# An identity product in each squaring, and full-width sums, in the recurrent stage of a hybrid decoder step

## The reference, cut to what matters

```python
def rwkv7_scan(r, decay, k, v, kk, kka, s0):
    def step(s, inp):
        r_t, w_t, k_t, v_t, kk_t, kka_t = inp
        s_kk = jnp.einsum('bhvk,bhk->bhv', s, kk_t)
        s = s * w_t[:, :, None, :] - s_kk[..., None] * kka_t[:, :, None, :] + v_t[..., None] * k_t[:, :, None, :]
        return s, jnp.einsum('bhvk,bhk->bhv', s, r_t)
    xs = tuple(jnp.swapaxes(t, 0, 1) for t in (r, decay, k, v, kk, kka))
    s_final, ys = lax.scan(step, s0, xs)
    return jnp.swapaxes(ys, 0, 1), s_final
```

## Time and profile before

| | us |
|---|---|
| median of 3 runs | 3478.74 |
| lowest, highest | 3476.14, 3480.61 |
| the profiled execution, its own time | 3477.89 |
| its span, first to last instruction | 3476.3 |
| the mean TensorE clock granted in it, of full | 0.943 |
| part of the span from the first `side` to the last (15 rounds) | about 2149.6 to 2624.3 |

### The profile page before, as it was taken

How to read it: one execution, slowest core, us unless ns; L and a number is a source line. 1 busy time by engine, 2 the same in 40 slices (tenths; PEclk the granted TensorE clock), 3 DMA queues, 4 the chain that set the end, 5 groups by cost and what they waited for, 6 DMA issues and landing times. The chain is left out here.

```text
span 3476.3 us, 65264 instructions
## 1 busy us (share of the span) xinstructions
PE 3178.0 (91%) x25272; PEld 1931.4 (56%) x25272; DVE 2175.2 (63%) x4350; ACT 1108.8 (32%) x2329; POOL 553.6 (16%) x782
## 2 busy tenths in 40 slices
PE   8999999999999999879999765877785999999998
PEld 4544445555555555446666544767774555555553
DVE  2018889999999999567666554777773344532221
ACT  4136650000000000145554325666652111111221
POOL 3330000000000000021011133445542000000000
PEclk9999999999999999979999876888877999999999
DMA  5232111121111111232111372222214312121110
GB/s 160 74 97 60 45 39 57 55 63 55 57 57 55 57 55 57 86 78 55 42 38 33 90 228 56 57 54 62 61 30 133 110 53 64 64 77 59 49 40 25
DMA packets 215814, 233.48 MB, mean 67 GB/s; under 512 B 28665, under 2 KB 191028, under 8 KB 215012
## 3 DMA queue, kind: packets, MB, share of 16 engines
q1 hardware_dynamic: 147960, 110.07, 11.7%
q0 software_dynamic: 23696, 59.79, 6.0%
q10 hardware_dynamic: 43868, 59.62, 4.9%
HBM read 158.75 MB, written 70.63 MB: 66 GB/s over the span
## 5 line engine op out<-in xcount | busy, mean ns | idle before, releaser
L409 PE MATMUL fro_acc<-h_t,fro_w 128*128 128x416 f32 x3280 | 1173.6, 515 | 0.0
L409 PEld LDWEIGHTS fro_acc<-h_t,fro_w 128*128 128x128 f32 x3280 | 614.2, 190 | 542.4 <-issue 535.5
L692 DVE TENSOR_SCALAR_CACHE_REDUCE fro_work<-scores,fro_real 128x384 uint8<-128x384 f32 (+6 forms) x462 | 656.2, 1474 | 2.1
L516 ACT ACTIVATE fro_out<-fro_acc 128x416 f32<-128x416 f32 (+3 forms) x230 | 118.0, 513 | 794.1 <-PE fro_acc L409 711.5
L3108 DVE CUSTOM_DVE_ANT_0 att_seen<-att_ps,scores 128x512 f32<-128x512 f32 (+3 forms) x320 | 181.4, 608 | 99.6 <-PE att_ps L2994 99.2
L2172 PE MATMUL mrg_po<-mrg_wo,mrg_mrg 128*128 128x512 f32 (+1 forms) x544 | 238.8, 597 | 4.6 <-DVE mrg_mrg L2277 4.6
L2204 PE MATMUL mrg_pg<-mrg_wg,mrg_x_t 128*128 128x512 f32 (+1 forms) x544 | 236.3, 592 | 0.0
L658 DVE SCALAR_TENSOR_TENSOR scores<-fro_work,w_idx,scores 128x512 f32<-128x512 f32 (+3 forms) x280 | 188.0, 671 | 39.2 <-ACT fro_work L573 12.2
L3078 ACT ACTIVATE att_seen<-att_seen,att_shift 128x128 f32<-128x128 f32 (+15 forms) x128 | 152.6, 1194 | 82.8 <-DVE att_shift L3116 82.8
L2172 PEld LDWEIGHTS mrg_po<-mrg_wo,mrg_mrg 128*128 128x128 f32 (+1 forms) x544 | 101.5, 187 | 139.1 <-issue 134.1
L573 ACT ACTIVATE fro_work<-fro_wk 128x512 f32<-128x512 f32 (+3 forms) x320 | 144.5, 540 | 90.7 <-PE fro_wk L482 89.8
(11 more groups left out here) (445 smaller groups left out, 4556.4 us busy)
## 6 DMA issues: line engine op xcount, KB each, us to landing
z_t<-fro_out ACTq DMA_DIRECT2D x180, 208.0 KB
fro_w<-in_w_in SPq DMA_DIRECT2D x41, 512.0 KB, 4.2
mrg_m_in<-z_t POOLq DMA_DIRECT2D x56, 256.0 KB, 3.3
scores<-in_cache_kv POOLq DMA_DIRECT2D x108, 128.0 KB, 3.2
rwk_zi<-z_t SPq DMA_DIRECT2D x80, 129.0 KB, 2.6
z_t<-fro_out ACTq DMA_DIRECT2D x45, 192.0 KB
scores<-in_x_prompt SPq DMA_DIRECT2D x16, 512.0 KB, 8.5
mrg_x<-in_x_prompt SPq DMA_DIRECT2D x16, 512.0 KB, 3.6
```

Of the source, the lines that this page charges most:

```text
L409: last = pe.matmul(acc[e % 2][:, 0:CW], w[block_no % 3][:, kk, :], h_t[:, kk, CW * g:CW * g + CW], start=(kk == 0), stop=(kk == KD - 1))
L692: chain.mark(dve.tensor_scalar(junk[b % 2][:, 0:n], scores[:, c:c + n], realf[:, b:b + 1], None, op, ALU.add, accum_out=count[:, b:b + 1]))
```

## The change

The sum of product and old series moves from DVE to PE: in `square(m, r)` for r from 1 to 4 each block's four products are followed by four products with `eye` that add the old series into the same place of PSUM. ACT then copies power and series together (`take_square`, 128x512 in place of 128x256), and DVE only transposes. The last series is copied by DVE in one instruction to `diag` (the room of `pw[0]`), transposed from there, and its first half is put into `inv` by a full-width product with a column of ones and zeros (`part`). The second half goes through PE: `corner` copies it by an identity product, and ACT takes both in one instruction. `first_product` is a full-width sum of two halves with such a column on DVE, behind the first transpose, and a full-width sum with the identity on POOL. `grams` now does all of e = 0 and then all of e = 1 with a semaphore after each, and `mask` waits for each half.

```diff
@@ first product
-                pool.wait_ge(masked, 4 * m + 4)
...
-                for i, (x, h) in enumerate(FOURTHS):
-                    w = fourth(x, h)
-                    pool.tensor_tensor(ta[1][w, :, 1, :], lower(gram[m % 2])[w, :, sub(h)], eye[w, None, :].to_broadcast([H, BLK, H]), ALU.add)\
-                        .then_inc(acc1_ok, 1)
-                    pool.wait_ge(acc1_ok, 4 * m + i + 1)
+                pool.wait_ge(acc1_ok, 2 * m + 1)
+                pool.tensor_tensor(ta[1][:, :, 1, :], ta[1][:, :, 1, :], eye[:, None, :].to_broadcast([P, BLK, H]), ALU.add).then_inc(acc1_ok, 1)
@@ grams
-                for i in range(2):
-                    for p2, x, e in HEADS:
-                        p = 2 * p2 + x
...
+                for e in range(2):
+                    if c:
+                        pe.wait_ge(masked, 4 * m + 1 + e)
+                    for i in range(2):
+                        for p2 in range(2):
+                            for x in range(2):
+                                p = 2 * p2 + x
...
+                    last.then_inc(grammed, 1)
@@ square
-                        last = pe.matmul(zz[w, 0, at], by, src, start=True, stop=True)
+                        last = pe.matmul(zz[w, 0, at], by, src, start=True, stop=(r == 0), skip_group_check=True)
+                    if r:
+                        for x, h in FOURTHS:
+                            w = fourth(x, h)
+                            last = pe.matmul(zz[w, 0, 64 * b + H:64 * b + 64], eye[w, :], ta[r % 2][w, b, 1, :], start=False, stop=True,
+                                             skip_group_check=True)
@@ corner
-                        last = pe.matmul(zz[fourth(x, 0), 0, 64 * b + H:64 * b + 64], ta[1][w, b, 0, :], inv[m % 2][w, b, sub(1)],
-                                         start=True, stop=True)
+                        pe.matmul(zz[fourth(x, 0), 0, 64 * b + H:64 * b + 64], ta[1][w, b, 0, :], diag[w, b, :], start=True, stop=True)
+                        last = pe.matmul(zz[w, 0, 64 * b + H:64 * b + 64], eye[w, :], diag[w, b, :], start=True, stop=True)
@@ take_square
+                    act.activation(ta[(r + 1) % 2][:, :, :, :].rearrange("p b i c -> p (b i c)"), zz[:, 0, :], ACT.Copy).then_inc(t_ok, 1)
@@ take_corner
-                for x in range(2):
-                    w = fourth(x, 0)
-                    act.activation(inv[m % 2][w, :, sub(1)], zz[w, 0, :].rearrange("p (b i c) -> p b i c", i=2, c=H)[:, :, 1, :], ACT.Copy)\
-                       .then_inc(inv_ok, 1)
+                if m >= 2:
+                    act.wait_ge(u_ok, NC * (m - 1))
+                act.activation(inv[m % 2][:, :, sub(1)], zz[:, 0, :].rearrange("p (b i c) -> p b i c", i=2, c=H)[:, :, 1, :], ACT.Copy)\
+                   .then_inc(inv_ok, 1)
@@ first_power
                 dve.transpose(pw[0][:, :, :], lower(gram[m % 2])).then_inc(p_ok, 1)
+                if m:
+                    dve.wait_ge(acc_ok, m)
+                dve.scalar_tensor_tensor(ta[1][:, :, 1, :], lower(gram[m % 2])[:, :, sub(1)], part[1][:, :], lower(gram[m % 2])[:, :, sub(0)],
+                                         ALU.mult, ALU.add).then_inc(acc1_ok, 1)
@@ power
-                    if r < 4:
-                        dve.tensor_tensor(ta[(r + 1) % 2][:, :, 1, :], got(r), ta[r % 2][:, :, 1, :], ALU.add).then_inc(acc_ok, 1)
-                        return
...
-                    for x, h in FOURTHS:
-                        w = fourth(x, h)
-                        last = dve.tensor_tensor(inv[m % 2][w, :, sub(h)], got(r)[w], ta[r % 2][w, :, 1, :], ALU.add)
...
+            def last_power(m):
+                dve.wait_ge(sq_ok, 5 * m + 5)
+                dve.tensor_copy(diag, zz[:, 0, :].rearrange("p (b i c) -> p b i c", i=2, c=H)[:, :, 1, :]).then_inc(acc_ok, 1)
+                dve.wait_ge(acc_ok, m + 1)
+                dve.transpose(pw[1][:, :, :], diag).then_inc(flipped, 1)
+                if m >= 2:
+                    dve.wait_ge(u_ok, NC * (m - 1))
+                dve.tensor_scalar(inv[m % 2][:, :, sub(0)], diag, part[0][:, :], None, ALU.mult).then_inc(inv_ok, 1)
```

More of the change, by code:

```diff
@@ L991, in stage_rwkv @@
         mask4, eye = s.sb("mask4", [P, 4 * C]), s.sb("eye", [P, H])
+        part = [s.sb(f"part{i}", [P, 1]) for i in range(2)]
         rheads = s.sb("rheads", [P, 4, P])
@@ L1013, in stage_rwkv @@
         inv = [s.sb(f"inv{i}", [P, BLK, C]) for i in range(2)]
+        diag = pw[0][:, :, 0:H]
         q_tok = [s.sb(f"q_tok{i}", [P, 2, 2, HD]) for i in range(2)]
@@ L1162, in _ @@
             pool.memset(e_in[:, :, :, 0:1], 1.0).then_inc(zeroed, 1)
-            for i in range(2):
-                pool.memset(inv[i][:, :, :], 0.0).then_inc(zeroed, 1)
             def shifted(m, i):
@@ L1336, in grams @@
                         pe.wait_ge(inv_ok, 2 * m)
-                else:
-                    pe.wait_ge(masked, 4 * m + 2)
-                for i in range(2):
-                    for p2, x, e in HEADS:
-                        p = 2 * p2 + x
-                        last = pe.matmul(zz[half_of(x), e, 256 * p2 + P * i:256 * p2 + P * i + P], kbz[half_of(e), i, p, tokens(c)],
-                                         ar[m % 3][half_of(e), p, c, :, :].rearrange("p a c -> p (a c)"), start=True, stop=True)
-                last.then_inc(grammed, 1)
+                for e in range(2):
[5 more added lines that the diff above has]
+                                p = 2 * p2 + x
+                                last = pe.matmul(zz[half_of(x), e, 256 * p2 + P * i:256 * p2 + P * i + P], kbz[half_of(e), i, p, tokens(c)],
+                                                 ar[m % 3][half_of(e), p, c, :, :].rearrange("p a c -> p (a c)"), start=True, stop=True)
+                    last.then_inc(grammed, 1)
             def square(m, r):
@@ L1351, in square @@
                 elif r == 1:
-                    pe.wait_ge(acc1_ok, 4 * m + 4)
-                else:
-                    pe.wait_ge(acc_ok, 4 * m + r - 1)
+                    pe.wait_ge(acc1_ok, 2 * m + 2)
                 low = lower(gram[m % 2])
@@ L1574, in exps @@
                 else:
-                    act.wait_ge(zeroed, 3)
+                    act.wait_ge(zeroed, 1)
                 act.activation(e_in[:, :, :, 1:C + 1], chunked(cum[:, :, :]), ACT.Exp, scale=decay_half()).then_inc(e_ok, 1)
@@ L1610, in take_square @@
                 act.wait_ge(sq_ok, 5 * m + r + 1)
-                act.activation(ta[(r + 1) % 2][:, :, 0, :], zz[:, 0, :].rearrange("p (b i c) -> p b i c", i=2, c=H)[:, :, 0, :], ACT.Copy)\
-                   .then_inc(t_ok, 1)
+                if r == 0:
+                    act.activation(ta[1][:, :, 0, :], zz[:, 0, :].rearrange("p (b i c) -> p b i c", i=2, c=H)[:, :, 0, :], ACT.Copy).then_inc(t_ok, 1)
+                else:
+                    act.activation(ta[(r + 1) % 2][:, :, :, :].rearrange("p b i c -> p (b i c)"), zz[:, 0, :], ACT.Copy).then_inc(t_ok, 1)
             def take_side(m):
@@ L1724, in _ @@
                 chain.mark(dve.tensor_copy(eye[w, :], k.ident[w, w]))
+            for h in range(2):
+                for x in range(2):
+                    for i in range(2):
+                        chain.mark(dve.memset(part[h][fourth(x, i), :], 1.0 if i == h else 0.0))
             for x in range(2):
@@ L1788, in scaled_keys @@
                 if m:
-                    dve.wait_ge(grammed, m)
+                    dve.wait_ge(grammed, 4 * m)
                     dve.wait_ge(kbt_ok, 2 * m)
@@ L1815, in first_power @@
                 dve.transpose(pw[0][:, :, :], lower(gram[m % 2])).then_inc(p_ok, 1)
[L1817 to L1818 removed]
+                if m:
+                    dve.wait_ge(acc_ok, m)
+                dve.scalar_tensor_tensor(ta[1][:, :, 1, :], lower(gram[m % 2])[:, :, sub(1)], part[1][:, :], lower(gram[m % 2])[:, :, sub(0)],
+                                         ALU.mult, ALU.add).then_inc(acc1_ok, 1)
             def power(m, r):
[L1822 to L1841 removed]
+                dve.wait_ge(t_ok, 4 * m + r + 1)
+                dve.transpose(pw[(r + 1) % 2][:, :, 0:H], ta[(r + 1) % 2][:, :, 0, :]).then_inc(p_ok, 1)
+            def last_power(m):
[6 more added lines that the diff above has]
+                dve.tensor_scalar(inv[m % 2][:, :, sub(0)], diag, part[0][:, :], None, ALU.mult).then_inc(inv_ok, 1)
             def take_u(n, c):
@@ L1942, in _ @@
                 if inverse:
-                    power(n + 1, 4)
+                    last_power(n + 1)
                 if features:
```

24 lines of the change are left out of this document (1 added, 23 removed).

## The result

The changed kernel takes 3525.08 us (median of 4 runs, 3514.93 to 3533.77), the kernel before, run beside it, 3479.68 (4 runs). The ratio is 1.0134, with a 95% interval from 1.0108 to 1.0159: 45 us slower, where 27 us faster was predicted. The profiled execution took 3522.3 us.

What follows compares the result with a forecast made beforehand. No engine is full; a round is a loop of waits, chiefly PE's for DVE and POOL. 10.11 + 19.19 = 29.30 us, plus 0.7 for the clock, gives 30.0 against 31.65, 25 us over 15 rounds: 3452 us, range 3428 to 3486.

Steps and rivals of the forecast that it cites:

- the price of the identity products: Squares 1 to 4 on PE: 32 identity products of 32 columns add 0.51 us to each square at full clock.
- M: Start of the mask of the second grams in a round; predicted at S + 10.11, 2.75 us sooner than before.
- The last sum: End of the squares on DVE: four instructions of 1.71 us become one copy of 0.41, so `side` starts at S + 0.95.
- `side` to the second grams: PE's stretch from `side`: 7.61 us with the clock kept; POOL is later and sets M at S + 10.11.
- S: Start of the last sum on DVE, the point from which a round's times are counted.
- Grams: The 16 products of a grams on PE in the new order: 1.94 us at full clock instead of 1.06.
- the rival that rested on it: Products sharing input rows do not run side by side: 16 take 3.6 us, about 3481 us, no change; chance 0.06.
- M to square 1: After the second mask starts: DVE's added sum and POOL's `pm` put the transpose at M + 5.71, square 1 at M + 6.2.
- Square 2: Start of square 2 on PE, behind ACT's wider copy of square 1: M + 11.10, 0.93 us later than before.
- Square 2 to the next S: Squares 2 to 4 at full clock: 6.78 us to square 4, then 1.31, so the next S is M + 19.19.
- The clock: PE's clock over a round: one fall to half in most rounds, 3 us long, taken as 0.7 us lost.
- The slower rival: Half clock stays behind `side` and PE's added work is paid double: 33.2 us a round, 3501 us; chance 0.12.

Runs made afterwards that it cites:

- the wide product: Changed kernel with one full 128x128 identity product over 256 columns replacing the 32 small ones in each of squares 1 to 4: 3449.64 us, ratio 0.9909.
- the one-column products: Kernel before plus 32 products of one column in each of squares 1 to 4, results overwritten before being read: 3575.99 us, ratio 1.0278.
- ident_alone: Kernel before with only the sum of squares 1 to 4 moved to PE, as 32 identity products each, and wide ACT copies: 3541.15 us, ratio 1.0172.
- one_ident_alone: Kernel before with only the sum of squares 1 to 4 moved to PE, as one full-width product each: 3474.06 us, ratio 0.9983.

## Why the prediction was wrong

The step that failed is the price of the identity products: "32 identity products of 32 columns add what a square of 32 columns takes beyond its start and end, 0.75 - 0.24 = 0.51". As the time of their columns that is right (0.50 at full clock where no stop falls in), but I never counted that they are 128 instructions a square, 512 a round. No rival priced instructions either. What the runs showed in its place are 60 stops of some 60 us in all, which go with the instructions. They are paid in the stretch after square 2 as idle time, and where one falls just ahead of `side`, the clock behind it is at half. Of the mean round, 34.3 us against 29.3 worked out at full clock, 2.3 us are lost ahead of M and 2.7 behind it. So the working up to M holds for the rounds that keep their clock and not for the mean.

- *The last sum.* Predicted one copy of 0.41; measured 0.42. By the row of the transpose, PE waited for it ahead of `side` once, 2.5 us at the last one (the waits above call this one "issue"), in place of 33.0 us in 16 rounds.
- *`side` to the second grams.* Predicted to keep its clock, with M at S + 10.11, set by POOL. In the round shown the clock is 1.00 from 2431 to 2436, the bias add ends at S + 3.89 (3.80 predicted), and M is S + 10.37. Ten of the 15 rounds do not keep their clock (0.50 to 0.88), and M is S + 10.6 to 18.4 in these. In the round shown `next_state` starts at 2440.53, 0.08 us after POOL's `keep_state` ended; the profile names PE's output product as the last to release it.
- *Grams.* Predicted 1.94 at full clock; from the first start (2439.88) to the last end it was 1.54. At half clock, as in most first `grams` of the changed kernel, it was some 2.8, where the prediction's 1.93 + 1.70 makes 3.6. Products that share input rows do run side by side, so the rule of the Trainium skill that I weighed against the earlier trace rows (TensorE: Matmul & The Clock Gate, "Part 3: Packing small matmuls") does not show here; the rival that rested on it fails.
- *M to square 1.* Predicted the transpose at M + 5.71 and square 1 at M + 6.2; measured M + 5.89 and M + 6.37. POOL's `pm` fell on DVE's new sum (1.43 us) rather than on `th_w` (0.41 then), the same collision on another instruction.
- *Square 2.* Predicted M + 11.10, behind ACT's copy; measured M + 10.88, behind it.
- *Square 2 to the next S.* Predicted 8.09 at full clock; measured 10.64, all of it at full clock. In this stretch lie three stops of 0.23, 1.13 and 0.85 us, one each 256 instructions, and a fourth of 1.53 follows behind S. With the 0.19 us that the record ahead of each hides (an estimate, from above) the three come to 2.8 us, the whole of the excess of 2.55.
- *The clock.* Predicted one fall in most rounds, 0.7 us; the mean rose from 0.83 to 0.88 only, and to 0.91 with the wide product. The slower rival (half clock stays behind `side`) came true in five rounds of 15, and in part in five more, but not for its reason: it hung on PE's wait for DVE, which is gone. Even with the wide product the clock isn't whole behind `side`: in 10 of 15 rounds it is 0.72 to 0.83 in these 6 us, as in this one, with PE busy throughout:

```profile
2396.30:2402.30 6.00, 6.00 (x170) 5.69 (x172) 4.03 (x8) 3.59 (x12) 3.20 (x3) 0.72 0.18 44
```

With the wide product the sum comes out: a round of 29.82 us where 30.0 was predicted, 3449.64 where 3452 was. That is the change as I had reasoned it, without the instructions that I had left out. Some of this agreement is luck: the last two rounds, which have less work in them, took 27.7 and 24.4 us, the 13 before them 30.4 in the mean, and the one fall of the clock that I had put around square 3 lies behind `side`.

What stays open: what sets the time of a block of instructions (no kernel changed anything about the queue itself); when the clock falls behind `side`; and why the one-column products cost some 97 us on top of the kernel before, where 32 products in place of a wide one cost 78 within the change and 66 without it (`ident_alone` against `one_ident_alone`).

## What to carry to other kernels

Price a small product on PE twice: by its columns, and by its instructions, of which a product of 4-byte numbers has four. Add up the instructions in the stretches where PE has no wait, and where 256 of them go by in less than some 4 us, look for "issue" ahead of products whose inputs have long been there. There one wide product over all rows in place of 32 tiled ones was worth 51 us of 3478; in squares 1 and 2, where PE waits for others anyway, the same count cost 17. And read more than one round before saying where a loop loses its time: the round shown here kept its clock behind `side`, and ten of the fifteen did not.

## What the runs showed of the hardware

- PE's instructions came in blocks of 256 (16 KB, 64 bytes each). In dense stretches of the changed kernel PE stopped for 0.2 to 2.3 us every 128 matmul records (256 with the weight loads), and these stops were 3.3 to 4.3 us apart.
- A product of one column and 32 rows took as long as one of 32 columns: 0.18 us for four of them beside four of 64 columns, at full clock.
- One identity product over 128 rows and 256 columns takes PE 0.53 us beyond the square ahead of it, about as much as 32 products of 32 rows and 32 columns (0.50 where no stop falls in), both at full clock.
- Products in four row groups that write one bank of PSUM run side by side: 32 of 64 columns took 1.09 us, where one after another they would take some 4.2 (an estimate from the 0.53 of the product of 256 columns). So do products with the same input rows and different output columns: 16 of 128 columns took 1.54 us, against 4.2 by the same estimate.
- DVE's full-width operation with two inputs from SBUF took 0.44 us with POOL at rest (2646.32) and 1.43 beside POOL's `pm` (2442.93), both in the changed kernel.
